# Splitting the first source rows of two output projections in the stage in front, and the low halves of a down projection between convolution taps

## The reference, cut to what matters

```python
# block 1, end of the mixing half
merged = sigmoid(ga) * (ret @ w_ret_o) + sigmoid(gb) * (att @ w_att_o)
x = x + gt_a[:, None, :] * (merged @ w_o)

# block 3, end of the mixing half: y_rwkv is a per-head group norm of the scan's
# output, scaled, plus a bonus times v, times a gate; then
y = concatenate([y_fox, y_rwkv, y_moba], axis=-1)
x = x + g1 * (y @ w_out)

# block 3, end of the kernel
u = causal_dwconv(h @ w_up, conv_w, conv_b)        # three taps per channel
u_gate, u_val = split(u, 2, axis=-1)
x = x + g2 * ((silu(u_gate) * u_val) @ w_down)
out = rms_norm(x, norm_final)
```

## Time and profile before

| | |
|---|---|
| median of 3 runs | 3697.02 us (3690.26 to 3699.26) |
| the profiled execution | 3691.89 us |
| its span in the trace | 3690.1 us |
| mean granted TensorE clock | 0.951 |
| PE busy | 3396.0 us, 92% of the span |
| DVE, ACT, POOL busy | 57%, 48%, 28% |
| DMA | 189 GB/s over the span |

### The profile page before, as it was taken

The page is one execution under the profiler, slowest core; times in us unless marked ns, Lnnn a source line. Parts: engine busy times, 40 slices in busy tenths (PEclk is TensorE's granted clock), DMA queues, the critical chain, the costliest instruction groups (busy, mean ns, idle before and its releaser), DMA issues. The chain is left out here.

```text
span 3690.1 us, 55627 instructions
## 1 busy us (share of the span) xinstructions
PE 3396.0 (92%) x20857; PEld 2751.7 (75%) x20857; DVE 2100.1 (57%) x2469; ACT 1755.6 (48%) x2294; POOL 1044.9 (28%) x435
## 2 busy tenths in 40 slices
PE   7989999979999999999999697899999977689997
PEld 5877777668888888888888573778887856668876
DVE  3320121279999999999999326421241155246665
ACT  3222333257777777778787434332233242133333
POOL 2334222213232323232323230134443300034443
PEclk9999999989999999999999898799999977899999
DMA  8223333359999999999999427123232200013221
GB/s 281 78 65 101 120 120 122 99 214 374 378 367 380 364 386 362 384 364 382 364 383 365 157 95 274 35 80 102 86 97 69 92 19 4 6 58 100 95 90 41
DMA packets 245516, 696.90 MB, mean 189 GB/s; under 512 B 17878, under 2 KB 149834, under 8 KB 186748
## 3 DMA queue, kind: packets, MB, share of 16 engines
q1 hardware_dynamic: 235196, 658.52, 48.1%
q0 software_dynamic: 9936, 36.18, 3.7%
q10 hardware_dynamic: 240, 0.12, 0.0%
HBM read 669.00 MB, written 30.23 MB: 189 GB/s over the span
## 5 line engine op out<-in xcount | busy, mean ns | idle before, releaser
L317 POOL TENSOR_TENSOR split_w<-ring,split_w 128x1024 fp32r<-128x1024 f32 (+1 forms) x294 | 699.6, 2380 | 1678.8 <-ACT split_w L312 1491.3
L2020 DVE TENSOR_TENSOR moe_low<-ring,moe_high 128x2048 fp32r<-128x2048 f32 x408 | 929.2, 2285 | 18.0 <-ACT moe_high L2010 16.9
L2010 ACT ACTIVATE moe_high<-ring 128x1024 fp32r<-128x1024 f32 x810 | 827.4, 1058 | 101.9 <-PE psum L2264 101.4
L312 ACT ACTIVATE split_w<-ring 128x1024 fp32r<-128x1024 f32 (+1 forms) x294 | 304.6, 1036 | 1029.8 <-PE psum L446 607.3
L2260 PE MATMUL psum<-moe_high,moe_xe 128*128 128x512 f32 x2176 | 585.0, 391 | 0.0
L2260 PEld LDWEIGHTS psum<-moe_high,moe_xe 128*128 128x128 f32 x2176 | 409.7, 188 | 83.9
L2171 POOL DMA_INDIRECT moe_y_rows<-moe_ye,moe_target x34 | 197.4, 5807 | 690.1 <-DVE moe_ye L2075 690.1
L446 PE MATMUL psum<-pair,split_w 128*128 128x512 f32 x1488 | 340.4, 391 | 4.3 <-PEq L3596 4.3
L2264 PE MATMUL psum<-moe_low,moe_xe 128*128 128x512 f32 x1088 | 336.3, 390 | 0.0
L446 PEld LDWEIGHTS psum<-pair,split_w 128*128 128x128 f32 x1488 | 281.1, 189 | 62.9 <-POOL split_w L317 4.4
L446 PE MATMUL psum<-b_pair,split_w 128*128 128x512 f32 x1392 | 322.1, 393 | 5.8 <-PEq L1249 2.6
(11 more groups left out here) (612 smaller groups left out, 4365.7 us busy)
## 6 DMA issues: line engine op xcount, KB each, us to landing
ring<-in_w_experts SPq DMA_DIRECT2D x408, 1024.0 KB, 7.9
ring<-in_w_mod SPq DMA_DIRECT2D x48, 1024.0 KB, 6.7
ring<-in_w_in SPq DMA_DIRECT2D x39, 1024.0 KB, 5.3
ring<-in_w_up SPq DMA_DIRECT2D x33, 1024.0 KB, 5.1
ring<-in_w_in SPq DMA_DIRECT2D x44, 512.0 KB, 5.3
ring<-in_w_down SPq DMA_DIRECT2D x20, 1024.0 KB, 5.0
ring<-in_w_gate SPq DMA_DIRECT2D x11, 1024.0 KB, 5.3
ring<-in_w_out SPq DMA_DIRECT2D x8, 1024.0 KB, 5.5
```

Source lines behind the costliest of these rows:

```text
L312: self.nc.scalar.activation(high, raw, ACT.Copy).then_inc(self.K.rounded, 1)
L317: self.nc.gpsimd.tensor_tensor(low, raw, high.bitcast(F32), ALU.subtract).then_inc(self.K.split, 1)
L2010: self.nc.scalar.activation(self.B["high"][:, j % HALVES, :], self.raw(j), ACT.Copy).then_inc(self.high, 1)
L2020: self.nc.vector.tensor_tensor(flat(self.low_of(j, 2)), self.K.ring[:, self.ring_slot(j // 2), :], high, ALU.subtract).then_inc(self.low, 2)
```

## The change

1. `SourceAhead` is new. In the stage in front of `w_o` and of `b3_out` it has ACT and POOL split the second weight place of the first chunk too, has ACT and DVE split pieces 0 and 1 of the source (rows 0 to 3), and has PE multiply piece 0 (`products`, 24 matmuls) at the end of that stage. The split source goes into the buffer of the block's `pair`, so the stage has no `w_o_a` or `b_out_a` of its own.
2. `rwkv_finish` is reordered: the gate's products come before v's transposes, ACT copies them to a new buffer `rf_gate`, the table for the square root is loaded ahead of the squares, and `b_vtok`'s multiply stands behind both variances. DVE's last multiplies read `rf_gate` in place of PSUM.
3. In `conv_up`, the low half of `b3_down`'s piece 2 comes behind tap 2 of the last unit, that of piece 3 behind tap 0. On ACT both steps stand ahead of the last sigmoid.
4. `Final` uses `ya`'s memory for its scratch and gain. No work changes by it.

```diff
+class SourceAhead(SplitAhead):
+    def part_of(self, i):
+        return self.own[:, :, 2 * (i % 4):2 * (i % 4) + 2, :]
+    def high(self, sc, i):
+        self.nc.scalar.activation(self.part_of(i)[:, 0, :, :], self.src[:, 2 * i:2 * i + 2, :], ACT.Copy)\
+            .then_inc(self.a_high, 1)
+    def low(self, ve, i):
+        ve.wait_ge(self.a_high, i + 1)
+        part = self.part_of(i)
+        self.nc.vector.tensor_tensor(part[:, 1, :, :], self.src[:, 2 * i:2 * i + 2, :], part[:, 0, :, :].bitcast(F32),
+                                     ALU.subtract).then_inc(self.a_split, 1)
+    def products(self, pe):
+        K, n, x = self.K, self.first, self.part_of(0)
+        pe.wait_ge(K.split, self.number(n, 0))
+        pe.wait_ge(self.a_split, 1)
+        w = K.w[:, 0, :, :].rearrange("p s (k n) -> p s k n", n=K.stream.chunks[n][0][0])
+        for t in range(NT):
+            for k in range(2):
+                for a, b in ((0, 0), (1, 0), (0, 1)):
+                    ins = self.nc.tensor.matmul(K.ps[:, t, :], x[:, a, k, t * P:(t + 1) * P], w[:, b, k, :],
+                                                start=(k + a + b == 0), stop=False)
+        ins.then_inc(K.first_used, 1)
...
 def attention_out(K, attT, merge, source):
...
             ahead.high_ahead(sc)
+            source.weights_high(sc)
+            sc.wait_ge(K.dve_evac, evac0 + 1)
+            for i in range(source.done):
+                source.high(sc, i)
...
+            source.weights_low(po)
...
+            pe.wait_ge(K.dve_evac, evac0 + 1)
+            source.products(pe)
...
                 merge(j, K.ps[:, 4 * j:4 * j + 4, :]).then_inc(K.dve_evac, 1)
+                if j == 0:
+                    for i in range(source.done):
+                        source.low(ve, i)
...
 def rwkv_finish(K, y, ya, R, col, out, source):
...
+                pe.wait_ge(gate_copied, RW_T)
+                source.products(pe)
...
+                sc.wait_ge(ya_copied, 2)
+                source.high(sc, 0)
+                for c in range(RW_T):
                     sc.wait_ge(v_turned, c + 1)
...
+                source.weights_high(sc)
+                sc.wait_ge(finished, 2)
+                source.high(sc, 1)
...
-                    nc.vector.tensor_tensor(out[:, 2 + c, :], ps[:, c, :], out[:, 2 + c, :], ALU.mult)
+                    nc.vector.tensor_tensor(out[:, 2 + c, :], gate[:, c, :], out[:, 2 + c, :], ALU.mult)\
+                        .then_inc(finished, 1)
+                ve.wait_ge(finished, 2)
+                source.low(ve, 1)
...
 def conv_up(K, stage, ctx, pair, cw, ffT):
...
+                    if j == units:
+                        follow(sc, 2, 4)
...
-            ins.then_inc(conv, 1)
+                if j == units - 1 and tap != 1:
+                    if not tap:
+                        ins.then_inc(conv, 1)
+                    follow(ve, 3 - tap // 2, 4 - tap // 2)
```

More of the change, by code:

```diff
@@ L463 @@
     free: Callable
+    begun: int = 2
 def linear_split(K, stage, kind, src, per_unit, act=None, dve=None, act_runs_ahead=2, paired=True, tiles=None,
-                 after=None, guests=(), lead=None, parts=None, hold=False, loads=None, onward=None):
+                 after=None, guests=(), lead=None, parts=None, hold=False, loads=None, onward=None,
+                 source=None):
     nc = K.nc
@@ L496, in linear_split @@
         per = len(order) // units
-        if not paired:
+        if source:
+            held, part_of, a_high, a_split = True, source.part_of, source.a_high, source.a_split
+        elif not paired:
             held = parts is None
@@ L506, in split_source @@
             n, place = order[i]
+            if source and i < source.done:
+                return
             r, nr = rows_of[n, place]
@@ L541, in step, with begin @@
                 loads.dve_step(eng, j, i)
-        begun = 2 if lead else 0
-        def begin(eng):
-            for n in range(begun):
+        begun = lead.begun if lead else 0
+        def begin(eng, lo=0, hi=2):
+            for n in range(lo, hi):
                 step(eng, None, n)
@@ L1173, in add_residual @@
     linear_split(K, stage, "N", src, per_unit, dve=dve, paired=False, tiles=tiles, after=after,
-                 guests=guests, lead=lead, parts=parts, loads=loads, onward=onward)
+                 guests=guests, lead=lead, parts=parts, loads=loads, onward=onward, source=source)
 RH, RDK, RDV = 4, 128, 256
@@ L2484, in merge @@
                                                            gb[:, 4 * j:4 * j + 4, :], ALU.add)
-                        attention_out(K, attT, merge)
+                        source = SourceAhead(K, "w_o", merged, pair, 2)
+                        attention_out(K, attT, merge, source)
             with ExitStack() as leave:
@@ L2498, in block1, with attention_out @@
         routing.close()
-def attention_out(K, attT, merge):
+def attention_out(K, attT, merge, source):
     nc = K.nc
     first, last = K.stream.span["att_o"]
-    ahead = SplitAhead(K, last)
+    ahead, evac0 = SplitAhead(K, last), K.dve_evac_n
     with nc.Block() as block:
@@ L3901, in _, with rwkv_finish @@
                 nc.vector.tensor_copy(y_last(1), y_bank(1)).then_inc(y_ready, 1)
-def rwkv_finish(K, y, ya, R, col, out):
+def rwkv_finish(K, y, ya, R, col, out, source):
     nc, ps, A = K.nc, K.ps, K.A
@@ L3940, in _ @@
                     ins.then_inc(v_turned, 1)
[L3941 to L3944, removed]
                 pe.wait_ge(v_ready, RW_T)
@@ L3971, in _ @@
                         sqrt(0)
-                    if c == 3:
+                    if c == 2:
                         sqrt(1)
+                    sc.wait_ge(gate_done, c + 1)
+                    nc.scalar.activation(gate[:, c, :], ps[:, c, :], ACT.Copy).then_inc(gate_copied, 1)
+                sc.wait_ge(ya_copied, 2)
+                source.high(sc, 0)
+                for c in range(RW_T):
                     sc.wait_ge(v_turned, c + 1)
@@ L4116, in block3 @@
             rwkv_scan(K, feat, R.beta, R.wend[:, :, :], R.vtok, y)
-            rwkv_finish(K, y, ya, R, col, K.hT)
-        with ExitStack() as ffn:
+            early.close()
             pair = K.sb(ffn, "b3_hpair", [P, 2, KD, S], F32R)
+            source = SourceAhead(K, "b3_out", K.hT, pair, 2)
+            rwkv_finish(K, y, ya, R, col, K.hT, source)
+        with ffn:
             taps = (Columns(K, "b3_cw01", [("0", A["conv_w_3"][0, 0]), ("1", A["conv_w_3"][0, 1])], ffn),
```

61 lines of the change are left out of this document (44 added, 17 removed).

## The result

| | before | changed |
|---|---|---|
| median of 5 runs | 3691.95 us (3690.26 to 3699.26) | 3675.59 us (3668.44 to 3678.57) |
| the profiled execution | 3691.89 us | 3668.44 us |
| its span | 3690.1 us | 3666.6 us |
| mean granted TensorE clock | 0.951 | 0.956 |

The ratio is 0.9950, with a 95% interval of 0.9940 to 0.9961: 16.4 us faster by the medians, 0.44%. The profiled execution is the fastest of the five, 7.2 us under its median, so its trace shows more gain (23.5 us of span) than the change has.

A forecast was written before the change was run, and what follows sets the result against it. The prediction took PE to bound the kernel, with only its gaps and slow stretches able to pay. Gains of 8.3 + 0.9 + 6.2 = 15.4 us, from a base of 3694.5, gave 3679 us, range 3672 to 3688 for 8 in 10.

The forecast's parts named there:

- What bounds: PE, busy 3396.0 of 3690.1 us; three gaps over 7 us behind DVE's low halves, each followed by slow products.
- Into `w_o`, 8.3 us: At `w_o`, PE's 7.42 us gap goes and piece 1 starts at 712.0 instead of 720.35; bounds 7.0 to 9.2.
- The stage's end: Ahead of `w_o`, the end of the stage in front costs PE about 1.3 us before piece 1 starts.
- Into `b3_out`, 0.9 us: At `b3_out`, stage in front 3.3 us longer, then PE waits for guests, yet gains 0.9 us; bounds -1.5 to +4.
- the guests' wait: At `b3_out`'s start, PE waits for four transfers, last issued at 3244.1 and landing 2.6 us later; PE stands 6 us.
- `b3_down`, 6.2 us: In `b3_down`, no gap before piece 2, 3.1 us before piece 3, clock kept; gain 6.2 us, bounds 4 to 7.5.
- piece 4's wait: In `b3_down`, piece 4's low half ends at 3565.7, 0.5 us after PE is ready.
- a clock that stays low: Sign of being wrong: the clock stays low where forecast high; in `b3_down` that takes 2 us of the gain.
- The sum: Over the three places, 8.3 + 0.9 + 6.2 = 15.4 us gained; likeliest 13 to 18 us, chance 0.62.
- The clock eats it: Rival: clock falls in `b3_down`'s 3.1 us gap too and `b3_out` gives nothing; 12.0 or 10.5 us, 3684; chance 0.17.
- The taps are not beaten: Rival: in `b3_down` PE stands 7 us behind piece 2, down projection gains nothing; 9.3 us, 3685; chance 0.08.
- Slower: Rival: guests' transfers at `b3_out` land late, each us beyond 2.6 costing 1; 0.3% slower at 26 more; chance 0.03.

The follow-up runs named there:

- e1_wo: The kernel before with the `w_o` part of the change alone; 3685.06 us, ratio 0.9984 to the runs of before.
- e8_weights: The changed kernel with `b3_out`'s second weight place split in the scan instead of in `rwkv_finish`; 3675.32 us.
- e5_guests: The changed kernel with the guests' four transfers issued at the start of `rwkv_finish` instead of in `b3_out`; 3671.85 us, beside 3677.47 for the changed kernel.
- e6: The changed kernel with one low half behind each of the three taps, and ACT's step for piece 4 ahead of the sigmoid; 3671.53 us.
- e7_both: The changed kernel with the edits of e5_guests and e6 together; 3667.61 us, ratio 0.9931 to the runs of before.

## Why the prediction was right, step by step

- **What bounds.** Right. The three gaps behind DVE's low halves were what the change could take, and it took one whole and most of another. The third, into `b3_out`, it exchanged for a wait on the guests' transfer. One reading in it is too high: "about 2.3 us of slow products" sets 7.72 us, from PE's start to ACT's restart, against 5.44, from one restart of ACT to the next. Measured alike, a piece at full clock takes 5.8 us (`w_o`'s piece 1 of the change), so the slow products cost 1.9.
- **Into `w_o`, 8.3 us.** Right in mechanism; 9.1 us at piece 1's start and 8.8 at its end. The stage's end was over-sized: 1.3 us forecast from rows with other stages, 0.47 measured. Behind it, counted from the first merge, 8.2 us are left at the experts over all 13 traces, so PE's chain carried the lead on nearly whole. e1_wo's time has 5.9 us, 3 to 9.
- **Into `b3_out`, 0.9 us.** The size was too small, but the sign and all four mechanisms were right: the longer stage in front (2.7 us measured, 3.3 forecast), POOL in DVE's way (e8_weights), PE's wait for the guests, and the slow piece behind it (7.33 us). The term that was mis-sized most is the guests' wait. I had PE wait for the last of four transfers, 1.1 us of issuing and then 2.6 of landing, and piece 1 start 3.8 us into the stage. PE could use the first 2.06 us after its issue and the last 2.81 us into the stage, 1.7 after its own issue, and piece 1 started 2.9 us in. With 0.9 us there, 0.6 by the stage in front and 0.5 by the slow piece (less 0.2 for the transposes), the gain by the first pair of traces was 2.7 us, and 3.9 by the means of three traces each.
- **`b3_down`, 6.2 us.** Measured 5.6 and 5.4 by the traces. The gap was shorter than forecast (2.56 against 3.1 us), since the taps, blocked once by POOL, ended at 3538.4 - 3520.6 = 17.8 us behind the first product, 18.3 forecast. But the clock was forecast to hold, because it had held behind 1.80 and 2.77 us. It fell in five of the six traces with this gap, at 1.3 to 1.6 us a time, and held in e5_guests. The half us that I had for piece 4's wait did not occur. So 0.5 + 0.5 of good luck met 1.5 of bad: the size is near by cancelling, and the clock, which I had high, was wrong. The prediction names a clock that stays low as a sign against it, and its bounds of 4 to 7.5 allow for it.
- **The sum**, 15.4 us: measured 16.4 by the medians, 14.8 to 18.8 by the ratios of three comparisons. `b3_out` gave more than forecast and `b3_down` less, so that the sum is this near is in part luck. 3679 was forecast, 3675.6 measured. Some of the 3.4 us between them is the base: I took the middle of before's four times at 3694.5, and its five runs have 3691.95.
- **The rivals.** "The clock eats it" was half there (the clock fell in `b3_down`), but `b3_out` gave more than nothing. "The taps are not beaten" is refuted by the gap of 2.56 us (its 9.3 us is 9.2 by the prediction's own terms). "Slower", by the guests' transfers, had its place right and its price small: e5_guests shows it to be worth 4 to 6 us, not 26.

Not settled: why the clock is kept behind a gap in one execution and lost in another. Nor is it known to better than a us or two what the edits of e5 and e6 are worth alone: the medians have 5.6 and 5.9 us, their traces 3.9 and 3.6, and e7_both 8.3 for the two together.

## What to carry to other kernels

When the first work of a stage is pulled into the stage in front, what stood second is now first, and each wait that it hid is bare: look there for transfers that are issued at the stage's own start, and issue them a stage sooner (3.9 us here by the trace). Count a PE gap together with the clock behind it, and where a gap of 2 to 3 us is left, work at closing it, since the 2.56 us gap here cost another 1.3 to 1.6 us in five of six traces. Measure a slow and a full-speed piece between the same two events. A trace that shows more gain than the medians is checked at points in code that did not change, before any cause is looked for.

## What was not expected of the hardware

The same gap kept the clock in one trace and lost it in another: 2.77 us ahead of the same product gave 0.23 us a product before and a granted clock of 0.67 in the changed kernel, and over all traces it kept the clock in four and lost it in nine. The 2.56 us gap lost it in five traces and kept it in one. Over 240 us of small products with many short gaps, the mean granted clock of identical code ran from 0.71 to 0.83, and its length from 235.0 to 251.2 us, which is more than the 15.9 us that the three parts of the change are worth.
